# Neighbourhood attention: pooling and turning first, then values, then scores, on all three engines

## The chip, the cores and the metric

The kernel runs on one core of one Trainium2 chip. The metric is the device time of one execution in microseconds (us). Five engines take part: TensorE (PE in the profile, with its weight loads as PEld), VectorE (DVE), ScalarE (ACT), GpSimd (POOL), and SyncE (SP), which issues most of the transfers.

## The reference, cut to what matters

The program is two transformer blocks over 256 tokens of width 1024, in float32. The first block has forgetting attention, a gated delta rule and a feed-forward net. The second block, where the change lies, mixes neighbourhood attention (8 heads of 64) with a pooling branch (4 groups of 128 columns), and then has a feed-forward net of its own:

```python
q = rms_norm(q, q_norm_g[l]); k = rms_norm(k, k_norm_g[l])
a = neighbourhood_attention(q, k, v, rpb[l])   # softmax(q k^T * scale + bias, in a window) v
p = multiscale_pool(u, w_pool[l], pool_scale[l])
x = x + jnp.concatenate([a, p], axis=-1) @ w_out[l]
...
def multiscale_pool(u, w_pool, pool_scale):
    # per group: (mean over a window of 2, 4, 8 or 16 tokens) - u
    y = jnp.einsum('btgc,gcd->btgd', d, w_pool).reshape(B, T, C)
    return y * pool_scale
```

## The kernel before

The order of all work is written by hand, with no scheduler. Each engine runs its own program (`tensor_program`, `scalar_program`, `vector_program`, `pool_program`, `sync_program`), and each program is one loop over the same 252 steps `n`. Step `n` of TensorE is one half panel of a large product (`gemm(n)`), and a few small jobs that hang on that step follow it. Weights come in panels into three buffers. ScalarE copies each half panel to its rounded high part (`panel_hi`, the `copy` at L1076) and VectorE subtracts it from the raw panel to get the low part (`panel_lo`, L1546). Both do this for step `n + 3` at the head of their step `n`, so weights are ready about three steps ahead. TensorE then multiplies high by high, low by high and high by low. All of its products are issued by one helper at L580, its turns (transposes) at lines of their own.

Around the change stand these steps. The panels of the second block's projections are `qk2` (two), `u2` and `v2`; `v2` ends at step 178, the output product `out2` takes steps 179 to 186. `NA_AT` (L191) hangs the 13 stages `v` of the attention on steps 172 to 182: stages 0 to 5 on steps 172 to 177, stages 6 and 7 both on step 178, stages 8, 9 and 10 on 179, 180 and 181, and 11 and 12 on 182. In a stage `v`:

- **scores** (`na_scores`, PE, even `v` below 8): two heads at a time, four products of q and k, each head into a bank of its own. It waits until both banks are free before its first product. VectorE (`na_bias`, L1903) adds the bias and takes the row minimum, which frees the bank; ScalarE (`na_exp`, L1309) takes the exponential one stage later, and VectorE (`na_normalise`, L1910 and L1913) divides two stages later.
- **turning** (`na_turn`, L941, head `v - 3`): four transposes; ScalarE (`na_turned`) copies the result to `na_pT` and frees the bank.
- **values** (`na_values`, by `VALUES_AT` at stages 7, 8, 10 and 12): eight products in the trace; ScalarE `na_hi` and VectorE `na_lo` (L1918) take the halves, and `na_lo` frees the bank.
- **pooling**: `pool_mean(g)` at stages 3 to 6 (band times u), which VectorE copies to `poolT` (L1923) and so frees the bank; `pool_out(g)` one stage later (poolT times wpool), of which ScalarE takes `mix_hi` (`pool_hi`) and VectorE then `mix_lo` (`pool_lo`, L1927), which frees the bank.

All these small results share four banks of PSUM, the ring `side` (banks 4 to 7). `bank_for` gives them out in the order in which TensorE's program asks, so the k-th job gets the bank of the job four before it, and waits until that one has been emptied:

```python
        rings = {"few": [0, 1], "fox": [2, 3], "side": [4, 5, 6, 7], "gemm": [0, 1, 2, 3]}
            n = rings[ring][ring_at[ring] % len(rings[ring])]
```

In stages 3 to 7 the ring is used in this order (one comma-separated job per bank): turn 0, mean 0; turn 1, scores 4, scores 5, out 0, mean 1; turn 2, out 1, mean 2; turn 3, scores 6, scores 7, out 2, mean 3; values 0, turn 4, out 3.

Of the kernel before, what the change touches and what calls it, by code (L numbers as in the profile page):

```python
# [28 lines left out]
HEADS = 8  # L29
# [163 lines left out]
VALUES_AT = {7: [0], 8: [1], 10: [2], 12: [3]}  # L193

POOL_AT = {3: 0, 4: 1, 5: 2, 6: 3}
# [5 lines left out]
def build(nc, a, out, scratch_a, scratch_x, scratch_c):  # L201
    ctx = ExitStack()
    with ctx:
# [374 lines left out]
        def tensor_program(e):  # L578
# [339 lines left out]
            def na_scores(pair):  # L918
                heads = (2 * pair, 2 * pair + 1)
                for hh in heads:  # L920
                    side(("na_s", hh))
                    for s, v in room(("na_s", hh)):
                        e.wait_ge(s, v)
                e.wait_ge(*emptied(("qk_turn", pair // 2, 0)))
                e.wait_ge(*emptied(("qk_turn", pair // 2, 1)))
                for m in range(TT):
                    for p0, hh in zip((0, NA_DIM), heads):
                        i_ = mm(pairs(bank_of(("na_s", hh)))[:, m, :],
                                q2T[p0:p0 + NA_DIM, pair, m * P:(m + 1) * P], k2T[p0:p0 + NA_DIM, pair, :])
                        if m == TT - 1:  # L930
                            i_.then_inc(will_fill(("na_s", hh)), 1)

            def na_turn(hh):
                key = ("na_t", hh)
                c3 = pairs(side(key))
                for s, v in room(key):
                    e.wait_ge(s, v)
                e.wait_ge(s_na_norm, hh + 1)
                for k in range(2):
                    for m in range(TT):  # L940
                        i_ = e.transpose(c3[:, k, m * P:(m + 1) * P], na_p[hh % 4][:, m, k * P:(k + 1) * P], ident)  # L941
                i_.then_inc(will_fill(key), 1)


            def na_values(pair):
                key = ("na_y", pair)
                bank = side(key)
                for s, v in room(key):
                    e.wait_ge(s, v)
                for m in range(TT):  # L950
                    e.wait_ge(*emptied(("v2", 0, m)))
                for hh in (2 * pair, 2 * pair + 1):
                    e.wait_ge(*emptied(("na_t", hh)))
                for k in range(2):
                    for p0, hh in ((0, 2 * pair), (NA_DIM, 2 * pair + 1)):
                        i_ = mm(bank[p0:p0 + NA_DIM, 0:T], v2[:, k, hh * NA_DIM:(hh + 1) * NA_DIM],
                                na_pT[hh % 4][:, k, :], k == 0, k == 1)
                i_.then_inc(will_fill(key), 1)

            def pool_mean(g):  # L960
                key = ("pool_m", g)
                bank = side(key)
                for s, v in room(key):
                    e.wait_ge(s, v)
                for m in range(TT):
                    e.wait_ge(*emptied(("u2", 0, m)))
                e.wait_ge(s_band, 16)
                gs = slice(g * P, (g + 1) * P)
                for m, to in enumerate((slice(0, P + POOL_REACH), slice(P - POOL_REACH, T))):
                    i_ = mm(bank[:, to], u2[:, m, gs], band[:, g, m, to], m == 0, m == 1)  # L970
                i_.then_inc(will_fill(key), 1)
# [20 lines left out]
            for n in range(1, STEPS + 1):  # L992
                gemm(n)
                if n == 1:
                    for j in range(2, 4):
                        e.wait_ge(s_h_act, j)
                        e.wait_ge(s_h_dve, j + 2)
                        turn_x("mix", j)
                if n in (15, 17, 25, 27):
                    gates_pe((15, 17, 25, 27).index(n))  # L1000
                if n - 6 in CONV_AT and CONVS[CONV_AT[n - 6]][0] == "q":
                    q_sums(CONV_AT[n - 6])
                if n - 5 in CONV_AT and CONVS[CONV_AT[n - 5]][0] != "q":
                    conv_turn(CONV_AT[n - 5])
                if n == 38:
                    e.wait_ge(s_gated, len(CONVS))
                    for b in range(4):
                        products_kk("kk", kT, b)
                if n == 40:
                    for b in range(4):  # L1010
                        products_kk("qk", qT, b)
                for b in range(2):
                    if n == 53:
                        px_16(b)
                    if n == 54:
                        xp_16(b)
                    if n == 55:
                        x_turn(b)
                    if n == 56:
                        px_32(b)  # L1020
                    if n == 57:
                        xp_32(b)
                    if n == 58:
                        x_turn2(b)
                    if n == 59:
                        px_64(b)
                    if n == 60:
                        xp_64(b)
                if n == 61:
                    solve_first()  # L1030
                if n == 62:
                    solve_state()
                if n == 63:
                    solve_second()
                if n == 64:
                    solve_out()
                if n == 76:
                    e.wait_ge(s_on, 2)
                    for b in range(4):
                        turn_units("yg", o_tok, b)  # L1040
                if n - 5 in FOX_AT:
                    fox_values(FOX_AT[n - 5])
                if n - 4 in FOX_AT:
                    fox_turn(FOX_AT[n - 4])
                if n in FOX_AT:
                    fox_scores(FOX_AT[n])
                for x, kind in (("ffn", "out"), ("norm1", "down"), ("norm2", "out2")):
                    for c in range(2):
                        if n == END[kind, c] + 1:
                            for m in range(TT):  # L1050
                                e.wait_ge(*emptied((kind, c, m)))
                            for j in (2 * c, 2 * c + 1):
                                turn_x(x, j)
                if n == END["out", 1] + 3:
                    row_factor("ffn", 2)
                if n == END["out2", 1] + 3:
                    row_factor("norm2", 5)
                if n - 4 in QK_AT:
                    for s_ in range(2):
                        qk_turn(QK_AT[n - 4], s_)  # L1060
                for v in NA_AT.get(n, ()):
                    for pair in VALUES_AT.get(v, ()):
                        na_values(pair)
                    if 0 <= v - 3 < HEADS:
                        na_turn(v - 3)
                    if v < HEADS and v % 2 == 0:
                        na_scores(v // 2)
                    if v - 1 in POOL_AT:
                        pool_out(POOL_AT[v - 1])
                    if v in POOL_AT:  # L1070
                        pool_mean(POOL_AT[v])


        def scalar_program(e):
# [294 lines left out]
            for n in range(1, STEPS + 1):  # L1369
# [146 lines left out]
                if n == END["v2", 0]:  # L1516
                    by_token("v2", 0)
                for v in NA_AT.get(n, ()):
                    for pair in VALUES_AT.get(v, ()):
                        na_hi(pair)  # L1520
                    if 0 <= v - 3 < HEADS:
                        na_turned(v - 3)
                    if 0 <= v - 1 < HEADS:
                        na_exp(v - 1)
                    if v - 1 in POOL_AT:
                        pool_hi(POOL_AT[v - 1])
                for kind, j in (("qk2", 0), ("qk2", 1), ("u2", 0)):
                    if n == END[kind, j]:
                        by_token(kind, j)
# [8 lines left out]
        def vector_program(e):  # L1538
# [448 lines left out]
            for n in range(1, STEPS + 1):  # L1987
# [213 lines left out]
                if n - 2 in QK_AT:  # L2201
                    qk_means(QK_AT[n - 2])
                for v in NA_AT.get(n, ()):
                    for pair in VALUES_AT.get(v, ()):
                        na_lo(pair)
                    if 0 <= v - 2 < HEADS:
                        na_normalise(v - 2)
                    if v < HEADS and v % 2 == 0:
                        na_bias(v)
                        na_bias(v + 1)  # L2210
                    if v - 1 in POOL_AT:
                        pool_lo(POOL_AT[v - 1])
                    if v in POOL_AT:
                        pool_mean(POOL_AT[v])
                if n - 3 in TAIL2_AT:
                    ffn2_lo(TAIL2_AT[n - 3])
                if n - 1 in TAIL2_AT:
# [266 lines left out]
```

## Time and profile before

| | us |
|---|---|
| three runs | 808.88, 809.01, 812.25 |
| their median | 809.01 |
| the profiled execution, device time | 809.28 |
| its span, first to last instruction | 808.0 |
| PE busy | 802.8 (99%) |
| PE weight loads busy | 724.0 (90%) |
| DVE busy | 592.0 (73%) |
| ACT busy | 449.8 (56%) |
| POOL busy | 75.3 (9%) |

A busy engine is one with an instruction running; consecutive instructions of one engine overlap, so the cost of a job is read from start to start, not from its own duration. In the timeline a row merges like instructions that follow each other: start, time until the last of them ends, engine, line, operation, what it writes and reads, and in brackets how long the engine was idle before it and on whom it waited. DMA engines are busy for about half of the span, and the stretch of the change lies between 576 and 612 us.

### The profile page before, as it was taken

The page shows a single profiled execution, that of the slowest core. Times are in us where ns is not written, and L with a number is a line of the kernel's source. Part 1 is how long each engine was busy: PE and PEld are TensorE (multiplying, and loading weights), DVE is VectorE, ACT ScalarE, POOL GpSimd, SP SyncE. Part 2 cuts the span into 40 slices and gives each one's busy share as a digit, 9 for nine tenths or more (in the row PEclk, how much of TensorE's full clock was granted, in tenths as well). Part 3 has the DMA queues.
Part 4 walks back from the last instruction along what each step waited for, and adds up shares of the span by engine and source line. Part 5 has one row for each costly group of instructions (what it writes and reads, how often), then busy time and mean ns, then how long its engine had stood idle before and what let it go on. Part 6 is the DMA issues. An engine that isn't in the chain of part 4 may idle for free.

```text
span 808.0 us, 14017 instructions
## 1 busy us (share of the span) xinstructions
PE 802.8 (99%) x5626; PEld 724.0 (90%) x5626; DVE 592.0 (73%) x993; ACT 449.8 (56%) x735; POOL 75.3 (9%) x65
## 2 busy tenths in 40 slices
PE   8999999999999999999999999999999999999998
PEld 6999998999999989899999998887778888888886
DVE  6888878875445776769999997486866777778543
ACT  6666577554535454546565663466665655655431
POOL 0001000010010402101111110011100111011000
PEclk9999999999999999999999999999999999999999
DMA  7855564647432554575688655465425656655541
GB/s 253 247 160 165 173 237 138 174 118 222 126 90 88 168 194 160 183 237 178 212 238 256 219 190 206 161 204 159 155 79 162 205 181 208 188 179 205 193 156 70
DMA packets 126113, 144.15 MB, mean 178 GB/s; under 512 B 11472, under 2 KB 102752, under 8 KB 125792
## 3 DMA queue, kind: packets, MB, share of 16 engines
q1 hardware_dynamic: 123744, 141.35, 54.6%
q10 hardware_dynamic: 2304, 1.90, 0.9%
q8 instruction: 45, 0.74, 0.4%
q14 instruction: 20, 0.16, 0.1%
HBM read 141.78 MB, written 1.46 MB: 177 GB/s over the span
## 4 chain that ended last, share of the span: by engine, by line
PE 98%; DMA 1%; DVE 1%; ACT 0%; issue 0%; ACTq 0%
PE bank L580 95%; DMA panel_raw<-in_w_in 1%; PE bank L634 1%; PE bank L941 0%; DVE panel_lo L1546 0%; PE bank L666 0%; PE bank L890 0%; ACT panel_hi L1076 0%; PE bank L914 0%; PE bank L721 0%; ACT x_halves L1076 0%; PE bank L823 0%; DVE h L1844 0%; DVE h L1978 0%; DVE zeros L1953 0%
## 5 line engine op out<-in xcount | busy, mean ns | idle before, releaser
L1546 DVE TENSOR_TENSOR panel_lo<-panel_raw,panel_hi 128x1024 fp32r<-128x1024 f32 x251 | 313.6, 1253 | 144.9 <-ACT panel_hi L1076 144.5
L580 PE MATMUL bank<-x_halves,panel_hi 128*128 128x256 f32 (+1 forms) x1952 | 416.0, 305 | 0.9 <-DVE x_halves L1973 0.7
L1076 ACT ACTIVATE panel_hi<-panel_raw 128x1024 fp32r<-128x1024 f32 (+1 forms) x253 | 266.5, 1056 | 163.5 <-PE bank L580 159.9
L580 PEld LDWEIGHTS bank<-x_halves,panel_hi 128*128 128x128 f32 x1952 | 315.7, 191 | 16.8 <-issue 0.9
L580 PE MATMUL bank<-x_halves,panel_lo 128*128 128x256 f32 x1152 | 324.8, 282 | 0.0
L580 PEld LDWEIGHTS bank<-x_halves,panel_lo 128*128 128x128 f32 x1152 | 219.8, 191 | 0.0
L580 PE MATMUL bank<-panel_hi,x_halves 128*128 128x512 f32 x256 | 80.6, 396 | 0.0
L580 PE MATMUL bank<-panel_hi,act_hi 128*128 128x512 f32 x176 | 68.6, 390 | 0.0
L580 PE MATMUL bank<-panel_hi,act_lo 128*128 128x512 f32 x176 | 68.5, 389 | 0.0
L580 PE MATMUL bank<-panel_lo,act_hi 128*128 128x512 f32 x176 | 68.5, 389 | 0.0
L580 PEld LDWEIGHTS bank<-panel_hi,x_halves 128*128 128x128 f32 x256 | 46.7, 188 | 9.9 <-DVE panel_lo L1546 0.6
L580 PE MATMUL bank<-panel_lo,x_halves 128*128 128x512 f32 x128 | 50.0, 391 | 0.0
L580 PEld LDWEIGHTS bank<-panel_hi,act_lo 128*128 128x128 f32 x176 | 33.0, 188 | 6.8
L580 PEld LDWEIGHTS bank<-panel_lo,act_hi 128*128 128x128 f32 x176 | 33.0, 188 | 6.8
L580 PEld LDWEIGHTS bank<-panel_hi,act_hi 128*128 128x128 f32 x176 | 33.0, 188 | 6.8
L2232 POOL TENSOR_TENSOR stats<-stats 128x2 f32<-128x2 f32 (+1 forms) x9 | 18.0, 2005 | 180.8 <-DVE stats L1560 102.1
L1580 DVE SCALAR_TENSOR_TENSOR conv_acc<-conv_tmp,params,conv_acc 128x255 f32<-128x255 f32 (+2 forms) x72 | 30.2, 477 | 0.0
L580 PEld LDWEIGHTS bank<-panel_lo,x_halves 128*128 128x128 f32 x128 | 24.0, 188 | 5.2
L2257 POOL TENSOR_TENSOR ff_tanh<-ff_tanh,ff_val 128x512 f32<-128x512 f32 x11 | 17.2, 1562 | 112.4 <-DVE ff_tanh L1870 112.4
L2237 POOL TENSOR_TENSOR key_bias<-key_bias,constants 128x128 f32<-128x128 f32 x16 | 9.4, 608 | 181.2 <-DMA key_bias<-gate_sums 181.2
L2264 POOL TENSOR_TENSOR f_tanh<-f_tanh,ff_val 128x512 f32<-128x512 f32 x11 | 14.3, 1300 | 108.3 <-DVE f_tanh L1946 108.3
L580 PE MATMUL bank<-yf_halves,panel_hi 128*128 128x512 f32 (+1 forms) x80 | 22.7, 350 | 0.0
(288 smaller groups left out, 937.1 us busy)
## 6 DMA issues: line engine op xcount, KB each, us to landing
panel_raw<-in_w_in SPq DMA_DIRECT2D x38, 1024.0 KB, 5.3
panel_raw<-in_w_up SPq DMA_DIRECT2D x30, 1024.0 KB, 5.3
panel_raw<-in_w_down SPq DMA_DIRECT2D x20, 1024.0 KB, 5.0
panel_raw<-in_w_gate SPq DMA_DIRECT2D x10, 1024.0 KB, 5.3
panel_raw<-in_w_out SPq DMA_DIRECT2D x8, 1024.0 KB, 5.0
panel_raw<-in_w_in SPq DMA_DIRECT2D x11, 512.0 KB, 4.8
panel_raw<-in_w_branch_fox SPq DMA_DIRECT2D x4, 1024.0 KB, 5.0
panel_raw<-in_w_branch_gdn SPq DMA_DIRECT2D x4, 1024.0 KB, 4.9
```

Of the source, the lines that this page charges most:

```text
L580: return e.matmul(o, l, r, start=start, stop=stop, skip_group_check=True)
L634: i_ = e.transpose(b3[:, k, m * P:(m + 1) * P], h[:, m, f * P:(f + 1) * P], ident)
L1076: return e.activation(o, i_, ACT.Copy, scale=scale)
L1546: e.tensor_tensor(lo, raw_view(i, k0, kt), hi.bitcast(F32), ALU.subtract).then_inc(s_lo, 1)
L1580: e.scalar_tensor_tensor(acc[:, f, back:], tmp[:, f, 0:T - back], gconv(p, f, back), acc[:, f, back:], ALU.mult, ALU.add).then_inc(s_taps, 1)
L2232: return e.tensor_tensor(cols, cols, minus_half.broadcast_to([P, n]), ALU.pow)
L2237: i_ = e.tensor_tensor(key_bias[:, s], key_bias[:, s], C("causal"), ALU.add)
L2257: e.tensor_tensor(th, th, ff_acc[j % 2][1], ALU.mult).then_inc(s_f_mul, 1)
L2264: e.tensor_tensor(th, th, ff_acc[j % 2][1], ALU.mult).then_inc(s_g_mul, 1)
```

## The change

In each stage, TensorE now does pooling (out, then mean), then the turn, then values, then scores. Before, it did values, turn, scores, then pooling. ScalarE and VectorE are put into a like order. No job moves to another stage, and no instruction is added or removed. Since banks are given out in the order of asking, the ring changes too. In stages 3 to 7 it is now: mean 0, turn 0; out 0, mean 1, turn 1, scores 4, scores 5; out 1, mean 2, turn 2; out 2, mean 3, turn 3, scores 6, scores 7; out 3, turn 4, values 0.

```diff
@@ tensor_program
                 for v in NA_AT.get(n, ()):
-                    for pair in VALUES_AT.get(v, ()):
-                        na_values(pair)
-                    if 0 <= v - 3 < HEADS:
-                        na_turn(v - 3)
-                    if v < HEADS and v % 2 == 0:
-                        na_scores(v // 2)
                     if v - 1 in POOL_AT:
                         pool_out(POOL_AT[v - 1])
                     if v in POOL_AT:
                         pool_mean(POOL_AT[v])
+                    if 0 <= v - 3 < HEADS:
+                        na_turn(v - 3)
+                    for pair in VALUES_AT.get(v, ()):
+                        na_values(pair)
+                    if v < HEADS and v % 2 == 0:
+                        na_scores(v // 2)
@@ scalar_program
                 for v in NA_AT.get(n, ()):
+                    if v - 1 in POOL_AT:
+                        pool_hi(POOL_AT[v - 1])
+                    if 0 <= v - 3 < HEADS:
+                        na_turned(v - 3)
                     for pair in VALUES_AT.get(v, ()):
                         na_hi(pair)
-                    if 0 <= v - 3 < HEADS:
-                        na_turned(v - 3)
                     if 0 <= v - 1 < HEADS:
                         na_exp(v - 1)
-                    if v - 1 in POOL_AT:
-                        pool_hi(POOL_AT[v - 1])
@@ vector_program
                 for v in NA_AT.get(n, ()):
-                    for pair in VALUES_AT.get(v, ()):
-                        na_lo(pair)
                     if 0 <= v - 2 < HEADS:
                         na_normalise(v - 2)
-                    if v < HEADS and v % 2 == 0:
-                        na_bias(v)
-                        na_bias(v + 1)
                     if v - 1 in POOL_AT:
                         pool_lo(POOL_AT[v - 1])
                     if v in POOL_AT:
                         pool_mean(POOL_AT[v])
+                    for pair in VALUES_AT.get(v, ()):
+                        na_lo(pair)
+                    if v < HEADS and v % 2 == 0:
+                        na_bias(v)
+                        na_bias(v + 1)
```

TensorE at stage 4 (step 176), as a difference. `poolT,wpool` is pool out 0, `band,u` mean 1, `na_p_139` turn 1, and `k2T,q2T` the scores of heads 4 and 5; the last row is the product of step 177.

```order
 L580 MATMUL bank<-panel_lo_60,x_halves 128x512
+L580 MATMUL bank<-poolT,wpool 128x256
+L580 MATMUL bank<-band,u_127 128x136 x2
 L941 MATMUL bank<-constants,na_p_139 128x128 x4
 L580 MATMUL bank<-k2T,q2T 128x256 x4
-L580 MATMUL bank<-poolT,wpool 128x256
-L580 MATMUL bank<-band,u_127 128x136 x2
 L580 MATMUL bank<-panel_hi_53,x_halves 128x512 x2
```

Pool out 0 and mean 1 moved ahead of the turn and the scores. Scores 5 is now the fourth job after out 0, and takes its bank.

TensorE at stages 6 and 7 (step 178), down to the first of the value products (`na_pT`), as a difference. `na_p_141` is turn 3, `na_p_138` turn 4, and the second `poolT,wpool` is out 3 of stage 7.

```order
 L580 MATMUL bank<-panel_lo_58,x_halves 128x512
+L580 MATMUL bank<-poolT,wpool 128x256
+L580 MATMUL bank<-band,u_127 128x136 x2
 L941 MATMUL bank<-constants,na_p_141 128x128 x4
 L580 MATMUL bank<-k2T,q2T 128x256 x4
 L580 MATMUL bank<-poolT,wpool 128x256
-L580 MATMUL bank<-band,u_127 128x136 x2
+L941 MATMUL bank<-constants,na_p_138 128x128 x4
 L580 MATMUL bank<-na_pT_142,v_126 64x256
```

Out 2 and mean 3 moved ahead of turn 3 and scores 6 and 7, and scores 7 takes the bank of out 2. Turn 4, which stood behind the values, stands ahead of them.

VectorE at stage 4, before: the second bias of head 5 (`na_p1`), then the low half of out 0, the copy of mean 1, and the weights of the next step.

```order
L1903 ISA na_p1_139,stats_150<-bank7,bias2_130 128x256
L1903 ISA stats_150 128x1
L1927 SCALAR_TENSOR_TENSOR mix_lo_137<-bank4,params_149,mix_hi_136 128x256
L1923 COPY poolT_133<-bank5 128x256
L1546 TENSOR_TENSOR panel_lo3_60<-panel_raw1_51,panel_hi3_56 128x1024
```

VectorE at stage 4, after: the division of head 2 (`na_p2`, two rows), then the same two pooling jobs, then the first bias of head 4 (`na_p0`). The file is a line longer, so line numbers are one higher.

```order
L1911 RECIPROCAL stats_150<-stats_150 128x2
L1914 TENSOR_SCALAR na_p2_140<-na_p2_140,stats_150 128x256 x2
L1928 SCALAR_TENSOR_TENSOR mix_lo_137<-bank5,params_149,mix_hi_136 128x256
L1924 COPY poolT_133<-bank6 128x256
L1904 ISA na_p0_138,stats_150<-bank4,bias2_130 128x256
```

The pooling jobs moved from behind the four bias instructions to ahead of them, right behind the division.

## Rows read from the trace of the kernel before

**Rows 1.** The page: span; and busy time of TensorE, share, instructions.
```profile
span 808.0 us, 14017 instructions
PE 802.8 (99%) x5626; PEld 724.0 (90%) x5626; DVE 592.0 (73%) x993; ACT 449.8 (56%) x735; POOL 75.3 (9%) x65
```

**Rows 2.** Waits of TensorE's weight loads on another engine, 592 to 594.5: total, times, longest.
```profile
PEld bank L941 <- DVE stats L1903: 0.4, 1, 0.4
```

**Rows 3.** Timeline of TensorE, stages 4 and 5 (steps 176 and 177).
```profile
580.10 0.60 PE L941 MATMUL bank<-constants,na_p 128*128 128x128 f32 x4
580.63 1.13 PE L580 MATMUL bank<-k2T,q2T 64*128 64x256 f32 x8
581.69 0.70 PE L580 MATMUL bank<-poolT,wpool 128*128 128x256 f32 x2
582.23 0.63 PE L580 MATMUL bank<-band,u 128*128 128x136 f32 x4
582.61 0.71 PE L580 MATMUL bank<-panel_hi,x_halves 128*128 128x512 f32 x2
...
585.89 0.60 PE L580 MATMUL bank<-poolT,wpool 128*128 128x256 f32 x2
586.33 0.63 PE L580 MATMUL bank<-band,u 128*128 128x136 f32 x4
```

**Rows 4.** Timeline of TensorE, stages 6 and 7 (step 178).
```profile
589.56 0.60 PE L941 MATMUL bank<-constants,na_p 128*128 128x128 f32 x4
...
592.25 1.08 PE L580 MATMUL bank<-na_pT,v 128*64 128x256 f32 x8
593.26 0.66 PE L941 MATMUL bank<-constants,na_p 128*128 128x128 f32 x4
...
594.01 0.58 PE L580 MATMUL bank<-panel_hi,mix_hi 128*128 128x512 f32 x1
```

**Rows 5.** Timeline of ScalarE, stages 3 to 6.
```profile
578.58 1.05 ACT L1076 ACTIVATE panel_hi<-panel_raw 128x1024 fp32r<-128x1024 f32 x1
...
582.43 0.47 ACT L1076 ACTIVATE mix_hi<-bank,params 128x256 fp32r<-128x256 f32 x1
...
586.09 0.60 ACT L1076 ACTIVATE na_pT<-bank 128x512 f32<-128x512 f32 x1 [2.24 <-PE bank L941]
...
587.57 0.46 ACT L1076 ACTIVATE mix_hi<-bank,params 128x256 fp32r<-128x256 f32 x1
587.93 1.05 ACT L1076 ACTIVATE panel_hi<-panel_raw 128x1024 fp32r<-128x1024 f32 x1
588.88 0.68 ACT L1076 ACTIVATE v<-bank,stats 128x512 f32<-128x512 f32 x1
```

**Rows 6.** Timeline of VectorE, stages 3 to 6.
```profile
577.81 0.16 DVE L1910 RECIPROCAL stats<-stats 128x2 f32<-128x2 f32 x1
...
578.53 0.42 DVE L1923 COPY poolT<-bank 128x256 f32<-128x256 f32 x1
579.66 1.23 DVE L1546 TENSOR_TENSOR panel_lo<-panel_raw,panel_hi 128x1024 fp32r<-128x1024 f32 x1 [0.71 <-ACT panel_hi L1076]
580.81 0.16 DVE L1910 RECIPROCAL stats<-stats 128x2 f32<-128x2 f32 x1
...
581.93 0.42 DVE L1903 CUSTOM_DVE_ANT_0 na_p<-bank,bias 128x256 f32<-128x256 f32 x1 [0.32 <-PE bank L580]
...
588.06 0.48 DVE L1927 SCALAR_TENSOR_TENSOR mix_lo<-bank,params,mix_hi 128x256 fp32r<-128x256 f32 x1 [2.08 <-ACT mix_hi L1076]
...
591.39 0.42 DVE L1903 CUSTOM_DVE_ANT_0 na_p<-bank,bias 128x256 f32<-128x256 f32 x1 [0.43 <-PE bank L580]
```

**Rows 7.** TensorE's opening products: the groups of 1 to 6 us, then the timeline.
```profile
L580 PE MATMUL bank<-zeros 128*128 128x512 f32 x6 | 5.5, 1088 | 1.4 <-DVE zeros L1953 1.4
...
8.78 1.02 PE L580 MATMUL bank<-zeros 128*128 128x512 f32 x2
11.33 0.47 PE L580 MATMUL bank<-x_halves,panel_hi 128*128 128x256 f32 x2 [0.66 <-DVE x_halves L1973]
```

## The prediction

> **What bounds the kernel now.** I read the page first: TensorE is busy for 802.8 of 808.0 us, and no other engine is near that [rows 1]. So the end is set by TensorE's own row of work. A change of order can take away only what TensorE waits, and can add whatever it makes TensorE wait. The second view is the waits, in the stretch of the attention. TensorE waits on another engine there once that the profile names, 0.4 us for a bank that the bias on VectorE empties [rows 2]. The timeline shows why the rest is dense: a stage's turn, scores, out and mean run start to start, in stage 4 at 580.10, 580.63, 581.69 and 582.23, with the next large product at 582.61 [rows 3]. The next thing to read is therefore the ring of four banks, with the order of stages 4 and 6: which job gets whose bank, and when that bank is emptied.
>
> **What goes.** No instruction goes. The waits that could go are the one of 0.4 us [rows 2] and a shorter one ahead of the values (they start at 592.25, and the bank they take is freed by the bias of head 6, which began at 591.39 [rows 4, 6]). That bounds the gain of the whole change at about 0.6 us, 0.07% of the time.
>
> **Stages 3, 5, 8 to 12.** The same jobs stand in another order within one step, and each finds its bank free: ring partners are a stage or more apart, and the jobs that empty them are done. Turn and values change places in stages 8 and 10, with a large product behind them, and nobody behind waits for either within a step. I take 0 for these. One side effect counts below: in stage 3 turn 0 stands behind mean 0, which costs 0.38 us start to start (582.23 to 582.61 [rows 3]), so ScalarE gets turn 0 0.38 us later, and its exponential and the copy of the high half behind that shift too. VectorE's split of that half began as the copy ended (578.58 + 1.05, then 579.66 [rows 5, 6]). It shifts to 580.04.
>
> **Stage 4: scores 5 waits for out 0, issued in the same step.** The bank of out 0 is free only when ScalarE has made the high half and VectorE the low half of it.
> - TensorE reaches the scores after out (0.44, 585.89 to 586.33), mean (0.38) and turn (0.53, 580.10 to 580.63) [rows 3]: 580.10 + 1.35 = 581.45.
> - ScalarE is early. Its work for out starts 0.74 after out does (581.69, 582.43 [rows 3, 5]), so by 580.84, and lasts 0.47.
> - VectorE is the late one. Its program puts the split and the division ahead of the low half. The split begins at 580.04; from split to reciprocal takes 1.15 (579.66 to 580.81), and from reciprocal to the instruction after the division 0.72 (577.81 to 578.53) [rows 6]. The low half starts at 581.91 and lasts 0.48 [rows 6], and with 0.08 for the signal the scores start at 582.47. That 0.08 is what is left where the values start at 592.25: bias from 591.39, two instructions of 0.35 and the read of the minimum [rows 4, 6].
> - So TensorE waits 1.02 us. Scores to the next job take 1.06 (580.63 to 581.69 [rows 3]), so the product of step 177 starts at 583.53, not 582.61: **+0.92 us**. The 0.10 between wait and loss is the slower start that out has behind the scores now (0.54 against 0.44).
>
> Behind the stalled scores on TensorE stands the product of step 177. Nothing hides the wait.
>
> **Stage 6: scores 7 waits for out 2, likewise.** The large product of step 178 ends at 589.56 + 0.92 = 590.48 [rows 4], and TensorE reaches the scores 1.35 later, at 591.83. On ScalarE the turn of stage 5 stands behind out 1 and mean 2: the step's first job now starts at 586.38, the turn at 587.20, and its copy 0.64 behind that, at 587.84, where it was 586.09. From there the exponential follows, and the high half of the weights comes 0.50 + 0.98 later (586.09 to 587.57 [rows 5], now with no pooling between), at 589.31, for 1.05. VectorE splits it from 590.39, divides from 591.54, and takes the low half of out 2 at 592.26 to 592.74. ScalarE has by then finished its part: after the weights it copies v twice and then makes the high half of out 2, at about 591.5 (0.95 for the weights, 588.88 - 587.93 [rows 5], and 0.6 for each copy). The scores start at 592.82, and TensorE has waited **0.99 us**.
>
> **Stage 7.** From there 1.06 for scores, 0.54 for out 3, 0.53 for turn 4, so the values are reached at 594.95. Their bank is that of scores 6, freed 0.86 after its bias starts (591.39 to 592.25 [rows 4, 6]), and that starts 1.30 after the scores (580.63, 581.93 [rows 3, 6]): 592.82 + 1.30 + 0.86 = 594.98. No wait to speak of: the turn and out 3 cover what was a short wait before. Values take 1.01 (592.25 to 593.26), and the output product starts at 595.99. Before, it started at 594.01, and by its long first record (0.58) some 0.1 later in effect [rows 4]: **+1.9 us in all**, with both waits and the small gains in it.
>
> **Does it come back?** All later work of TensorE stands in a row behind this, and nothing in it waits for a transfer in this stretch, so the 1.9 us stay. VectorE's and ScalarE's splits slip by up to 1.7 us, but they run about three steps ahead: the split that began at 589.01 serves step 181. That is covered by two large products of 2.8 us and the small jobs. Without that cover each us of slip would be a us of the end.
>
> **Sum.** 809.28 (profiled execution) + 1.9 = 811.2. The median of the runs is 0.27 lower than the profiled one, so I put the forecast at **810.9 us**, +0.23%. Bounds of the two unseen waits: at least 0.3 each, if VectorE is free when ScalarE is done (out 0.74, then 0.49 to the low half, 587.57 to 588.06, then 0.48 + 0.08, is 1.79 from out's start, less 1.35; 0.44, or 0.1 less by the start after scores), and at most 1.4 each, if the slip of one feeds the other. That is +0.4 to +2.8 with the gains of 0.2 at the low end.
>
> **Rivals.**
> 1. *No wait to speak of* (809.0). The low half would come early enough, or the order of the banks would not bite. Against it: the bank numbers of the built order (out 0 and scores 5 in one bank), and the 1.35 us of PE work between them, less than the bare chain of 1.79. It also holds if a slack that I missed takes the loss back. Chance 0.14.
> 2. *A small gain* (808.7): the banks come free in time and the named waits go, -0.3. It needs rival 1 and more. Chance 0.04.
> 3. *The clock falls* (816.9, slower by over 0.5%). TensorE would be at the lower of its levels (1.2 instead of 2.4 GHz) after each wait, which stands between transposes and small products. The opening shows what that level costs: six products of 128x512 took 1088 ns each, while two of the same at 8.78 were over in 1.02 us together [rows 7]. If the large product behind each wait (2.85 us) runs at half speed, that is 5.7 us more: 811.2 + 5.7. It decides as soon as a wait of 1 us is enough to lower the clock. Against it: at 11.33 TensorE had been idle for 0.66 us, right behind eight transposes, and the products there ran at full speed [rows 7]. Chance 0.04. The Trainium skill, "TensorE: Matmul & The Clock Gate", section "A second HAM failure mode: psum-queue depth-cycling", says that a kernel whose matmul groups pause often while cycling through PSUM banks can lose its clock again and again; by that, the time would be this rival's. The trace speaks for no such thing at 0.66 us; at 1.0 us no row of it can tell.
> 4. *The slip reaches the large products* (about 814, slower by 0.6%): a late split starves one of steps 179 to 182. It decides at a slip of over 4 us, and I find 1.7. Chance 0.03.
>
> **How the numbers follow.** The forecast of two waits has 0.75. A measurement of this kernel can tell about 0.5% (4 us) from no change. The forecast and rivals 1 and 2 all lie within it; outside are rivals 3 and 4 and a stray median (one of three runs was 812.25). Faster 0.02, within 0.5% 0.90, slower 0.08. The range takes rival 1 at its low end and the upper bounds with a little spread of the median at its high end: 809.0 to 812.7.
>
> **What would show it.** In the profile of the changed kernel: PE waits named by the low half of out (L1928) ahead of the scores in stages 4 and 6, of about 1 us each; the low half of out 0 right behind the division on VectorE; the values with no wait; the output product about 1.9 us later than 594.01; a granted clock of 1.00 there. The forecast is wrong if those scores start without a wait, if the low half waits for ScalarE and not for VectorE's own row, or if the loss is gone again at the end.

## The result and the profile after

The changed kernel takes 811.48 us (median of 14 runs, 811.12 to 812.12) against 809.38 us (14 runs of the kernel before beside it, 808.88 to 812.45). The ratio is 1.0019, with a 95% interval of 1.0010 to 1.0028: slower by 0.2%, which is real and small. The forecast was 810.9 us, in a range of 809.0 to 812.7.

The page of the changed kernel: span and busy time. The work is the same as in [rows 1], the span is 2.1 us longer, and TensorE's busy time is not.

```profile
span 810.1 us, 14017 instructions
PE 802.5 (99%) x5626; PEld 724.2 (89%) x5626; DVE 591.7 (73%) x993; ACT 450.5 (56%) x735; POOL 75.7 (9%) x65
```

So what came in is waiting. The chain of work that ended last, of the changed kernel, has two pieces in this stretch that no instruction of TensorE fills (start, length, what):

```profile
581.15 0.44 PE bank L941 x4
581.59 0.95 issue
582.54 4.98 PE bank L580 x26
...
591.60 0.44 PE bank L941 x4
592.04 0.96 issue
593.00 1.76 PE bank L580 x10
```

The timeline of TensorE, changed kernel, stages 3, 4, 6 and 7, to be read against [rows 3, 4]:

```profile
576.43 0.62 PE L580 MATMUL bank<-band,u 128*128 128x136 f32 x4
...
580.09 0.59 PE L580 MATMUL bank<-poolT,wpool 128*128 128x256 f32 x2
580.52 0.63 PE L580 MATMUL bank<-band,u 128*128 128x136 f32 x4
580.99 0.60 PE L941 MATMUL bank<-constants,na_p 128*128 128x128 f32 x4
582.54 1.13 PE L580 MATMUL bank<-k2T,q2T 64*128 64x256 f32 x8 [0.95 <-issue]
583.60 0.73 PE L580 MATMUL bank<-panel_hi,x_halves 128*128 128x512 f32 x2
...
593.00 1.13 PE L580 MATMUL bank<-k2T,q2T 64*128 64x256 f32 x8 [0.96 <-issue]
594.06 0.70 PE L580 MATMUL bank<-poolT,wpool 128*128 128x256 f32 x2
594.60 0.60 PE L941 MATMUL bank<-constants,na_p 128*128 128x128 f32 x4
595.13 1.08 PE L580 MATMUL bank<-na_pT,v 128*64 128x256 f32 x8
596.14 0.50 PE L580 MATMUL bank<-panel_hi,mix_hi 128*128 128x512 f32 x1
```

The scores of stages 4 and 6 are the jobs that wait. The profile names nobody for it ("issue"). VectorE's timeline of the changed kernel does: the low halves of out 0 and out 2 end at 581.96 + 0.48 = 582.44 and 592.42 + 0.48 = 592.90, and the scores start 0.10 us behind each.

```profile
580.09 1.23 DVE L1547 TENSOR_TENSOR panel_lo<-panel_raw,panel_hi 128x1024 fp32r<-128x1024 f32 x1 [1.17 <-ACT panel_hi L1077]
581.23 0.16 DVE L1911 RECIPROCAL stats<-stats 128x2 f32<-128x2 f32 x1
581.43 0.62 DVE L1914 TENSOR_SCALAR na_p<-na_p,stats 128x256 f32<-128x256 f32 x2
581.96 0.48 DVE L1928 SCALAR_TENSOR_TENSOR mix_lo<-bank,params,mix_hi 128x256 fp32r<-128x256 f32 x1
...
592.42 0.48 DVE L1928 SCALAR_TENSOR_TENSOR mix_lo<-bank,params,mix_hi 128x256 fp32r<-128x256 f32 x1
```

**The measure used below.** The time of whole runs moves by up to 4 us (808.69 to 812.69 in 35 runs of the kernel before), a good part of it in the opening (last section), which is more than most edits here cost. So each profile is also read by one distance on TensorE: from its first small job of stage 3 (576.43 here) to the first matmul of the output product (596.14 here). For the kernel before it is 17.55 us, from 576.46 to 594.01 [rows 4], for the changed one 19.71: **+2.16 us**. Where out stands right ahead of the output product, that product's first record is long (0.58 for 0.50), and 0.1 us of the distance is hidden in it. Each distance is read from one profile. What speaks for it is the rest of the span: from the output product to the last instruction twelve of the thirteen profiles take 213.94 to 214.16 us, so a loss in the distance is a loss at the end. The thirteenth is "before, outs in other banks" with 215.08, whose loss lies behind the distance.

| kernel | distance, us | against before | median, us | before beside it |
|---|---|---|---|---|
| before | 17.55 | | 809.38 | |
| changed | 19.71 | +2.16 | 811.48 | 809.38 |
| turn first | 17.71 | +0.16 | 809.70 | 809.60 |
| low half first | 18.65 | +1.10 | 810.49 | 809.60 |
| low half last | 20.38 | +2.83 | 812.21 | 809.60 |
| outs in other banks | 17.92 | +0.37 | 809.78 | 809.60 |
| new order in stages 0 to 4 | 18.62 | +1.07 | 810.78 | 809.42 |
| new order in stages 5 to 12 | 18.71 | +1.16 | 810.53 | 809.42 |
| ScalarE and VectorE alone | 21.50 | +3.95 | 813.63 | 809.42 |
| VectorE alone | 19.24 | +1.69 | 812.70 | 809.60 |
| ScalarE alone | 20.22 | +2.67 | 812.56 | 809.60 |
| before, outs in other banks | 17.53 | -0.02 | 810.42 | 809.42 |
| changed, longer wait | 27.14 | +9.59 | 819.17 | 810.06 |

The medians alone do not part every row from the kernel before: the 95% interval of the ratio is 0.9998 to 1.0026 for low half first, and begins at 1.0000 for both halves of the new order. What is said of losses near 1 us rests on the profiles.

### The profile page after: what moved, and what is told of

Same layout as the page of the kernel before. It is cut to its first block, busy times and chain, and to the rows that moved or that the text cites. A ratio compares the mean times of both kernels' runs of the same rounds, so it can differ in the third digit from the quotient of the medians.

```text
span 810.1 us, 14017 instructions
## 1 busy us (share of the span) xinstructions
PE 802.5 (99%) x5626; PEld 724.2 (89%) x5626; DVE 591.7 (73%) x993; ACT 450.5 (56%) x735; POOL 75.7 (9%) x65
## 4 chain that ended last, share of the span: by engine, by line
PE 97%; DMA 1%; DVE 1%; ACT 0%; issue 0%; ACTq 0%
PE bank L580 95%; DMA panel_raw<-in_w_in 1%; PE bank L634 1%; DVE panel_lo L1547 0%; PE bank L666 0%; PE bank L941 0%; PE bank L890 0%; ACT panel_hi L1077 0%; PE bank L914 0%; PE bank L721 0%; ACT x_halves L1077 0%; PE bank L823 0%; DVE h L1845 0%; DVE h L1979 0%; DVE zeros L1954 0%
```

## Experiments on the changed kernel: whose wait it is

**Turn first.** The diff against the changed kernel, TensorE and ScalarE:

```diff
+                    if 0 <= v - 3 < HEADS:
+                        na_turn(v - 3)
                     if v - 1 in POOL_AT:
                         pool_out(POOL_AT[v - 1])
                     if v in POOL_AT:
                         pool_mean(POOL_AT[v])
-                    if 0 <= v - 3 < HEADS:
-                        na_turn(v - 3)
@@
-                    if v - 1 in POOL_AT:
-                        pool_hi(POOL_AT[v - 1])
                     if 0 <= v - 3 < HEADS:
                         na_turned(v - 3)
+                    if v - 1 in POOL_AT:
+                        pool_hi(POOL_AT[v - 1])
```

> The changed kernel, but with the turn ahead of out and mean on TensorE, and its copy ahead of out's high half on ScalarE. Scores are still last and VectorE's order is that of the changed kernel. The ring gives scores 5 and 7 the banks of turn 1 and turn 3, which ScalarE alone frees. Theory (the wait for out's bank is the whole loss): no wait ahead of the scores, the output product starts at about 594.1 us instead of 596.1, time 809.4. Rival B (it is TensorE's order of kinds, pooling ahead of scores, that costs): about 811.3. Rival C (the new order on the other two engines costs): 810.5 to 811.5.

Measured: 809.70 us, ratio to before 1.0003 (0.9989 to 1.0016), and the loss of 2.16 us is down to 0.16. TensorE's timeline in this kernel, stage 6: the scores follow mean 3, which carries no idle time in brackets.

```profile
589.29 0.60 PE L941 MATMUL bank<-constants,na_p 128*128 128x128 f32 x4
589.73 0.60 PE L580 MATMUL bank<-poolT,wpool 128*128 128x256 f32 x2
590.16 0.63 PE L580 MATMUL bank<-band,u 128*128 128x136 f32 x4
590.77 1.13 PE L580 MATMUL bank<-k2T,q2T 64*128 64x256 f32 x8
```

Pooling still stands ahead of the scores, VectorE's order is untouched, and the bank of scores 7 is now that of turn 3, freed by ScalarE alone. Rival B falls, and rival C as far as it is VectorE's order. ScalarE's was changed here too, so for ScalarE the next run decides. It is not the kinds in a row, it is whose bank the last job of the stage inherits.

**Outs in other banks.** All orders of the changed kernel are kept:

```diff
-        rings = {"few": [0, 1], "fox": [2, 3], "side": [4, 5, 6, 7], "gemm": [0, 1, 2, 3]}
+        rings = {"few": [0, 1], "fox": [2, 3], "side": [4, 5, 6, 7], "gemm": [0, 1, 2, 3], "spare": [0, 1]}
@@ pool_out
-                bank = side(key)
+                bank = bank_for("spare", key)
```

> The changed kernel with all orders kept, but the four outs write to banks 0 and 1, which stand empty in these stages, and not to the ring. Theory: no wait ahead of the scores, since out no longer shares a bank with them, and none ahead of the values either; output product at about 593.9 us, time 809.2. Rivals B and C: the loss stays, 811 to 811.5.

Measured: 809.78 us, loss 0.37. The scores do not wait. What is left is a wait of 0.22 us that I had not expected, ahead of out 3. The profile names nobody for it. On VectorE the copy of mean 3, which out 3 reads, ends at 591.34 + 0.41 = 591.75, 0.10 us before out 3 starts:

```profile
590.50 1.13 PE L580 MATMUL bank<-k2T,q2T 64*128 64x256 f32 x8
591.85 0.67 PE L580 MATMUL bank<-poolT,wpool 128*128 128x256 f32 x2 [0.22 <-issue]
```

The order on its own does not make the loss: with the same order on all three engines and no sharing of a bank between out and scores, 1.8 of the 2.16 us go, and rival C falls for ScalarE as well.

**Low half first, and low half last.** Two opposite moves on VectorE:

```diff
-                    if 0 <= v - 2 < HEADS:
-                        na_normalise(v - 2)
                     if v - 1 in POOL_AT:
                         pool_lo(POOL_AT[v - 1])
+                    if 0 <= v - 2 < HEADS:
+                        na_normalise(v - 2)
@@ and the other kernel
-                    if v - 1 in POOL_AT:
-                        pool_lo(POOL_AT[v - 1])
                     if v in POOL_AT:
                         pool_mean(POOL_AT[v])
+                    if v - 1 in POOL_AT:
+                        pool_lo(POOL_AT[v - 1])
```

> The changed kernel with one move on VectorE: the low half of out stands ahead of the division instead of behind it. Theory (VectorE's own row ends the wait): the wait of stage 4 falls from 0.95 to about 0.2 us, that of stage 6 from 0.96 to about 0.5 (there ScalarE's high half is then the last to come), time 810.3. If ScalarE's high half or the bare chain were what ends the waits, nothing changes: 811.5.

> The changed kernel with the opposite move on VectorE: the low half of out stands behind the copy of mean. Theory: each of the two waits grows by the 0.4 us of the copy, to about 1.35 us, time 812.3. Rival (the wait is not VectorE's row): unchanged, 811.5.

Measured: 810.49 and 812.21 us. The rows of the scores in TensorE's timeline, stages 4 and 6, first of low half first:

```profile
581.93 1.14 PE L580 MATMUL bank<-k2T,q2T 64*128 64x256 f32 x8 [0.23 <-issue]
...
592.04 1.14 PE L580 MATMUL bank<-k2T,q2T 64*128 64x256 f32 x8 [0.61 <-issue]
```

and of low half last:

```profile
583.04 1.14 PE L580 MATMUL bank<-k2T,q2T 64*128 64x256 f32 x8 [1.27 <-issue]
...
593.85 1.14 PE L580 MATMUL bank<-k2T,q2T 64*128 64x256 f32 x8 [1.28 <-issue]
```

The waits follow VectorE's row in both directions: 0.95 and 0.96 become 0.23 and 0.61, or 1.27 and 1.28. Their sum falls by 1.07 and the distance by 1.06, or rises by 0.64 and 0.67. So every part of such a wait is a loss of the whole kernel, and VectorE's own row sets its end. In stage 6 of low half first a longer part is left, as expected of ScalarE's high half: there VectorE itself stands idle for 0.29 us ahead of the low half, waiting for it.

**The new order in stages 0 to 4 alone, or from stage 5 on alone.** All three engines get both orders and a condition, `v <= 4` in one kernel and `v >= 5` in the other. On TensorE:

```diff
+                    if v <= 4:
+                        if v - 1 in POOL_AT:
+                            pool_out(POOL_AT[v - 1])
...
+                    else:
+                        for pair in VALUES_AT.get(v, ()):
+                            na_values(pair)
...
```

> The new order on all three engines in stages 0 to 4, the old one from stage 5 on. Theory: one wait of 0.95 us, in stage 4 alone, so about half the loss: the product of step 177 at 583.6 us, time 810.3. If the two waits are one loss that the second stage would have had anyway: 811.4 or 809.4.

> The old order up to stage 4, the new one from stage 5 on. Theory: one wait of about 1 us, in stage 6 alone; time 810.4, and the losses of this run and of the one with stages 0 to 4 add up to that of the changed kernel.

Measured: +1.07 and +1.16 us of distance, and one wait each, 0.95 in stage 4 and 0.96 in stage 6. Together 2.23 against the 2.16 of the changed kernel. The two losses add up, and one is not the cause of the other. The median of the first (810.78) came out 0.5 above the expected 810.3; its distance did not.

## Experiments on the kernel before: what each engine's order costs alone

**ScalarE and VectorE in the new order, TensorE in the old one.** The edit is the second and third part of the change.

> Only the other two engines have the new order; TensorE's is that of before. Theory: the scores start without a wait, but on VectorE the bias of head 6 now stands behind the low half of out 2 and the copy of mean 3, which TensorE issues after the scores. So the bank of scores 6 comes free 1.7 us later, and the values wait for it: they start at about 594.0 us instead of 592.25, time 811.0. Rival (ScalarE's and VectorE's orders are off the path): 809.4.

Measured: 813.63 us, ratio 1.0052 (1.0035 to 1.0070), loss 3.95 us. More than double what was expected, and more than the whole change costs. The view of TensorE's waits in this kernel (who waited for whom, total us, times, longest):

```profile
PE bank L580 <- ACT na_pT L1076: 2.1, 2, 1.1
...
PE bank L580 <- DVE stats L1903: 1.2, 1, 1.2
```

The third wait was forecast, ahead of the values. The first two were not. I had traced VectorE's row, and had taken ScalarE for one with slack, which it has: 56% busy. But its new order puts the high half of out 0 ahead of its copy of turn 1, and with TensorE's old order out 0 is issued two jobs behind the turn. ScalarE stands and waits for out, with the turn ready. Mean 1 has the turn's bank, so TensorE waits behind that. To part the two, each engine's order was run alone.

**VectorE alone, ScalarE alone.**

> The kernel before, with the new order on VectorE alone. The run with the new order on both other engines lost 4.1 us where 1.7 were expected; its trace shows three waits on TensorE, 1.20 us ahead of the values and 1.05 us ahead of each of means 1 and 3. Theory: the wait ahead of the values is VectorE's (the bias of head 6 behind the copy of mean 3), the other two are ScalarE's. Here then the values alone wait: they start 1.7 us later against the turn of stage 3 than in the kernel before, time 811.1, and no mean waits. If the three waits hang together: 813.6 or 809.4.

> The kernel before, with the new order on ScalarE alone. Theory: ScalarE's high half of out 0 now stands ahead of its copy of turn 1, and TensorE issues out 0 two jobs behind the turn; mean 1 has the bank of turn 1 and waits 1.05 us for that copy, and mean 3 that of turn 3. The product of step 177 starts 1.2 us later, the output product 2.4 us, time 811.8, and this loss and that of the run with VectorE alone add up to about 4.1. Rival (ScalarE has slack): 809.4.

Measured: losses of 1.69 and 2.67 us. TensorE's timeline, stages 6 and 7 of VectorE alone:

```profile
594.78 0.63 PE L580 MATMUL bank<-band,u 128*128 128x136 f32 x4
597.05 1.08 PE L580 MATMUL bank<-na_pT,v 128*64 128x256 f32 x8 [1.64 <-DVE stats L1903]
```

and of ScalarE alone:

```profile
593.88 0.70 PE L580 MATMUL bank<-poolT,wpool 128*128 128x256 f32 x2
595.63 0.73 PE L580 MATMUL bank<-band,u 128*128 128x136 f32 x4 [1.05 <-ACT na_pT L1076]
596.29 1.08 PE L580 MATMUL bank<-na_pT,v 128*64 128x256 f32 x8
```

Each has only its own wait. The 1.69 is what was worked out (1.7). An idle time of 1.05 is a loss of 1.21: out to mean is 1.75 start to start here, and 0.54 without a wait [rows 3]. Idle time is counted from the modelled end of the matmul before, the loss from start to start. That much was expected (1.2 for each). The 2.67 is 0.3 more, mainly because mean to the next job is 0.1 longer behind a wait (584.85 to 585.33, against 0.38 [rows 3], and 595.63 to 596.29, against 0.56 in the kernel before). The two losses add to 4.36, a little more than the 3.95 of both together: where means 1 and 3 wait already, the values wait less (1.20 instead of 1.64). The medians of these two kernels (812.70 and 812.56) are above the expected 811.1 and 811.8 by more than the distance accounts for; the profile of each shows an early weight transfer that lands late (last section).

So the three parts of the change belong together. TensorE's new order takes away all three waits that the new orders of the others make, and brings two of its own.

**The kernel before, outs in other banks.** The two-line edit from above, made to the kernel before.

> The kernel before, with the four outs in banks 0 and 1 instead of the ring. Theory: the ring no longer forces the short wait ahead of the values, so the output product starts some 0.2 us earlier, time 809.2, which is not to be told from the kernel before. If ring waits that the profile doesn't name cost more than that: 808.8 or less.

Measured: 810.42 us, ratio 1.0014 (1.0003 to 1.0026): slower, against both readings. The distance is unchanged (17.53), but from the output product's start to the values of stage 8 it now takes 4.11 us, from 596.72 to 600.83, where the kernel before takes 3.01 (594.01 to 597.02). The view of TensorE's waits names it:

```profile
PE bank L580 <- DVE mix_lo L1927: 0.8, 1, 0.8
```

Out 3 is the last job ahead of the output product in the old order, and sits in bank 1, which is the second bank of that product. These banks are spare only until step 179. In the changed kernel with the same edit there are turn 4 and values 0 in between, and the product's first 2.86 us (593.90 to 596.76) show no such wait. The short waits of the kernel before turned out to be worth nothing that could be measured. The one ahead of the values was none: they start 0.56 us behind the mean there (591.69 to 592.25) and also here (594.40 to 594.96), where they take the bank of turn 3 and not that of scores 6.

**No version beats the kernel before.** Turn first and the changed kernel with outs in other banks come level with it (ratios of 1.0003).

## A longer wait: does the clock fall?

The third rival of the prediction was a clock that falls behind the waits. The waits of 0.95 to 1.28 us did not bring it. So they were made longer, with filler work on VectorE ahead of the low half in stages 4 and 6, on a scratch tile:

```diff
+                    if v in (4, 6):
+                        done = 0 if v == 4 else 2
+                        if done:
+                            e.wait_ge(s_filler, done)
+                        e.memset(filler, 0.0).then_inc(s_filler, 1)
+                        e.wait_ge(s_filler, done + 1)
+                        e.tensor_tensor(filler, filler, filler, ALU.add).then_inc(s_filler, 1)
                     if v - 1 in POOL_AT:
                         pool_lo(POOL_AT[v - 1])
```

> The changed kernel with filler work on VectorE ahead of the low half of out 0 and out 2, nothing else changed: a fill and an addition of a scratch tile of 128x1024, which together should take about 2.0 us (1.2 for the addition, as for the split of a half panel). Each wait ahead of the scores grows from 0.95 to about 3.0 us. Theory (a wait costs its own length): the output product starts 4 us later than in the changed kernel, time 815.5. Rival 3 of the prediction (the clock falls behind a wait): it was wrong for waits of 1.0 to 1.3 us, but in other runs TensorE ran at half speed behind an idle time of 2.5 us in the opening. If it does so here, the scores and the first matmuls behind each wait take up to twice as long, some 1 to 1.5 us more per wait, time 817.5 to 818.5.

Measured: 819.17 us, ratio 1.0125 (1.0105 to 1.0145). TensorE's timeline in this kernel, around both waits:

```profile
584.93 1.13 PE L582 MATMUL bank<-k2T,q2T 64*128 64x256 f32 x8 [3.28 <-issue]
586.00 0.73 PE L582 MATMUL bank<-panel_hi,x_halves 128*128 128x512 f32 x2
...
597.72 2.08 PE L582 MATMUL bank<-k2T,q2T 64*128 64x256 f32 x8 [3.29 <-issue]
599.73 1.22 PE L582 MATMUL bank<-poolT,wpool 128*128 128x256 f32 x2
600.74 1.06 PE L943 MATMUL bank<-constants,na_p 128*128 128x128 f32 x4
601.73 1.98 PE L582 MATMUL bank<-na_pT,v 128*64 128x256 f32 x8
603.64 0.61 PE L582 MATMUL bank<-panel_hi,mix_hi 128*128 128x512 f32 x1
```

and its stretches (length; busy us and instructions of PE, PEld, DVE, ACT and POOL; granted clock; DMA share; GB/s):

```profile
583.00:590.00 7.00, 5.07 (x29) 4.22 (x30) 5.43 (x17) 1.69 (x4) 0.00 (x0) 1.00 0.07 4
...
597.00:604.00 7.00, 6.28 (x23) 3.79 (x24) 3.50 (x15) 0.72 (x2) 0.00 (x0) 0.51 0.01 2
```

Two waits of one length, 3.28 and 3.29 us, and two outcomes. Behind the first the scores take 1.13 us and the clock stays at 1.00. Behind the second the scores take 2.08, everything up to 603.64 runs at twice its time, and the granted clock is 0.51, which is the lower level, 1.2 GHz. From the second scores to the output product are 5.92 us there against 3.14 in the changed kernel (593.00 to 596.14), so the lower clock costs 2.8 us beside the wait. It was already low before the scores began: 1.00 up to 597.0, 0.63 from 597.0 to 597.3, then 0.50. Of the 7.43 us by which the distance outgrows that of the changed kernel, 4.66 are the longer waits and 2.78 the clock. All four runs of this kernel have the same mean granted clock, 0.996, so the profiled run is not an odd one. The rival's mechanism exists, and a wait of 1 us does not reach it here. How long a wait must be is not settled by this.

## Why the prediction was right

- **What bounds the kernel** held: TensorE's busy time is unchanged (802.8 and 802.5 us), and the waits went to the end in full. The distance grew by 2.16, the span by 2.1 and the median by 2.1 us. Nothing gave it back.
- **Stage 4.** Forecast: a wait of 1.02 us, scores at 582.47, +0.92. Measured: 0.95, 582.54, and the product of step 177 at 583.60, +0.99. VectorE's row came as worked out: split 580.09 for 580.04, low half 581.96 for 581.91. TensorE's row was off a little: mean to turn takes 0.47 (580.52 to 580.99), where I had 0.38 from mean to a large product. So TensorE came later, and the idle time is shorter, but the loss is not: what counts is when the scores start.
- **Stage 6.** Forecast 0.99 and scores at 592.82, measured 0.96 and 593.00. The 0.18 is the 0.07 from stage 4 and 0.1 from the same cause: turn 2 came later behind mean 2, its copy on ScalarE with it, and so the split on VectorE (590.55 for 590.39).
- **Stage 7.** The values start 1.07 us behind out 3 (594.06 to 595.13), as worked out. In place of "no wait to speak of" a trace of one is left (0.2 us of a weight load on VectorE).
- **The sum**: +1.9 forecast, +2.1 measured by the medians. The bounds of +0.4 to +2.8 held it. The time itself came out 0.6 us above the forecast of 810.9, and 0.4 of that is the base: 809.01 from three runs, 809.38 from 14. With 14 runs a side the interval is 0.09% wide each way, so 0.2% could be told from nothing, where the prediction had put the limit at 0.5%.
- **What the profile would show**: the waits are there, but "issue" stands where I had said it would name the low half. The kernel with the low half moved, and the row of VectorE, show the cause that the label does not.
- **Rival 1** was out by the chain of 1.79 against 1.35 us. **Rival 2** fell too: the waits of the kernel before were worth under 0.1 us even where out had left the ring (a distance of 17.53 for 17.55). The prediction misread one of them. The values of stage 7 did not start at 592.25 because of the bias of head 6, so the 0.08 us "for the signal" that was worked out there was near the measured 0.10 by luck. The gains of 0.2 us in the low bound and the size of this rival also rest on such waits, and no run shows them. **Rival 3** was named with a real mechanism and rightly held unlikely: the granted clock is 1.00 from 570 to 612 us, with two waits of about 1 us beside transposes. By the section of the Trainium skill that was named with it ("TensorE: Matmul & The Clock Gate", "A second HAM failure mode: psum-queue depth-cycling") frequent short pauses could have been enough; it gives no length for one, and the two of 0.95 and 0.96 us in this trace were not. The price of 2.85 us for a fall was close to the 2.8 that one cost behind the wait of 3.29 us, though over other jobs. **Rival 4** did not occur: no large product from step 177 to 182 shows idle time. One weight load, at 600.54, is put down to a split (0.39 us), but the product starts as close behind the values as in the stage before (1.02 us, and 1.01 at 596.14). The 0 for stages 8 to 12 held too: output product to end is 213.99 us before and 213.96 in the changed kernel.
- Where I was wrong was in expectations of the experiments: ScalarE's order in the run with the two engines alone, and the bank 1 of the output product. Both are one mistake. I followed the engine on which I expected the wait and did not walk the others' rows through the same steps.

## What to carry to other kernels

When several small jobs share a ring of buffers and there are more jobs in a step than buffers, the last job of the step takes the buffer of one issued in the same step. So put the job whose buffer is freed by the shortest chain first (here the turn, which one engine empties). Out, which two engines empty one after the other, cost 2.16 us in that place, the turn 0.16. An engine at half load can still hold up the busiest one: what counts is what stands ahead of the releasing instruction in its own order, so a change of order on three engines is to be walked through on all three.

## What the runs showed of the hardware

- **The opening differs from run to run by more than the change is worth.** In some profiles one of the early weight transfers takes 2 us longer to land, and TensorE waits for the low half that hangs on it. That link of the chain that ended last (start, length), in the kernel before, and in VectorE alone:

```profile
15.65 6.12 DMA panel_raw<-in_w_in
```

```profile
15.26 8.32 DMA panel_raw<-in_w_in
```

  The waits that follow are 0.27 and 2.48 us. The profiled run with 2.48 took 814.08 us, where the lowest of that kernel's 12 runs took 810.48. The link takes 7.80, 7.92 and 7.96 us in ScalarE alone, in the kernel before with outs in other banks, and in the new order of stages 0 to 4, with waits of 1.96, 2.07 and 2.11 us. The runs of the kernel before differ by as much (808.88 to 812.45), but its profile shows the short wait alone, so that it is the same cause there is likely and not shown. Part of the spread goes with the clock: of the 29 runs of the kernel before beside the two kernels with the order split by stages, the six slowest (811.81 to 812.32) have a mean granted clock of 0.998, and the other 23 (810.76 at most) one of 1.00. It does not set the time alone: of the 21 runs beside VectorE alone two with 0.998 took 810.11 and 810.30. Where in those six it fell, no trace shows. Why the transfer is late was not tried.
- **The clock falls in the opening as well, behind a wait of 2.48 us.** TensorE's timeline in VectorE alone:

```profile
26.02 0.77 PE L580 MATMUL bank<-x_halves,panel_hi 128*128 128x256 f32 x2 [2.48 <-DVE panel_lo L1546]
...
26.80 0.63 PE L580 MATMUL bank<-x_halves,panel_hi 128*128 128x256 f32 x2
...
27.44 0.63 PE L580 MATMUL bank<-x_halves,panel_hi 128*128 128x256 f32 x2
...
30.32 0.40 PE L580 MATMUL bank<-x_halves,panel_hi 128*128 128x256 f32 x2
...
30.68 0.40 PE L580 MATMUL bank<-x_halves,panel_hi 128*128 128x256 f32 x2
```

  Three matmuls of 256 columns take 0.64 us start to start behind it (26.80 to 27.44) and 0.36 later on (30.32 to 30.68), and the granted clock is 0.50 from 26 to 28 us. In the other openings an idle time of 2.07 us was followed by the lower clock as well (0.50 from 27 us; before with outs in other banks), and ones of 2.11 and 1.96 us were not (1.00 throughout; stages 0 to 4, and ScalarE alone). Of the two of 3.3 us above one was. So one profile without a fall does not show that a wait is safe from it.
- **Idle time is not the loss.** A wait of 1.05 us in brackets cost 1.21 us start to start, and a turn behind a mean starts 0.09 us later than a large product does.
